# Weight sums of w_down made in place, products reordered, and seven products for two more tiles of gate and up

## The reference

```python
h = rms_norm(x, norm2[l])
x = x + (jax.nn.silu(h @ w_gate[l]) * (h @ w_up[l])) @ w_down[l]
return rms_norm(x, final_norm)
```

## Time and profile before

| | us |
|---|---|
| median of 3 runs | 660.89 |
| lowest, highest | 660.51, 661.07 |
| the profiled execution | 662.12 |
| its span, first to last instruction | 660.3 |
| TensorE busy | 646.7 (98% of the span) |
| VectorE busy | 451.1 (68%) |
| ScalarE busy | 348.5 (53%) |
| GpSimd busy | 265.0 (40%) |
| TensorE's granted clock, mean | 0.998 of full |

### The profile page before, as it was taken

One profiled execution on the slowest core, in us unless ns is written; L12 is line 12 of the kernel. 1 busy time (PEld: TensorE's weight loads), 2 busy tenths in 40 slices (PEclk: granted clock), 3 DMA queues, 4 the chain that ended last, 5 costly groups with the idle time before them and its releaser, 6 DMA issues.

```text
span 660.3 us, 11056 instructions
## 1 busy us (share of the span) xinstructions
PE 646.7 (98%) x3915; PEld 569.7 (86%) x3915; DVE 451.1 (68%) x929; ACT 348.5 (53%) x689; POOL 265.0 (40%) x158
## 2 busy tenths in 40 slices
PE   8999999999999999999999999999999999999996
PEld 7988988898899887888877888899999998888884
DVE  5435447555655687634489988469688797788894
ACT  7546446688665378715332362344444446655663
POOL 4766253674242440224466767344444320000222
PEclk9999999999999999999999999999999999999999
DMA  8989959469794993144699999887677858766553
GB/s 243 270 180 255 280 150 246 124 181 372 218 256 117 246 172 65 32 161 117 160 297 293 294 281 284 216 228 222 189 230 216 255 177 268 253 201 197 185 172 127
DMA packets 114774, 139.22 MB, mean 211 GB/s; under 512 B 5044, under 2 KB 74784, under 8 KB 114720
## 3 DMA queue, kind: packets, MB, share of 16 engines
q1 hardware_dynamic: 97880, 107.35, 51.9%
q0 software_dynamic: 14176, 26.64, 22.5%
q10 hardware_dynamic: 2664, 4.53, 2.0%
HBM read 132.19 MB, written 54.81 MB: 283 GB/s over the span
## 4 chain that ended last, share of the span: by engine, by line
PE 82%; issue 8%; POOL 6%; DVE 2%; ACT 1%; DMA 1%; POOLq 0%; SPq 0%; DVEq 0%; ACTq 0%
PE bank L776 8%; PE bank L778 8%; PE bank L777 8%; PE bank L795 7%; PE bank L797 7%; PE bank L796 7%; PE bank L1107 6%; PE bank L1105 6%; PE bank L1106 6%; PE bank L948 6%; POOL w_lo L728 4%; PE bank L924 3%; PE bank L908 2%; PE bank L909 2%; POOL down_sums L746 1%
## 5 line engine op out<-in xcount | busy, mean ns | idle before, releaser
L728 POOL TENSOR_TENSOR w_lo<-raw,w_hi 128x1024 fp32r<-128x1024 f32 (+1 forms) x76 | 191.6, 2525 | 259.4 <-ACT w_hi L1148 258.8
L1148 ACT CAST w_hi<-raw 128x1024 fp32r<-128x1024 f32 (+1 forms) x141 | 144.1, 1028 | 148.3 <-PE bank L1107 32.2
L795 PE MATMUL bank<-xT_hi,w_hi 128*128 128x512 f32 x272 | 109.0, 401 | 1.6 <-POOL w_lo L728 1.4
L797 PE MATMUL bank<-xT_hi,w_lo 128*128 128x512 f32 x272 | 107.0, 393 | 0.0
L796 PE MATMUL bank<-xT_lo,w_hi 128*128 128x512 f32 x272 | 106.7, 392 | 0.0
L1774 DVE TENSOR_TENSOR w_lo<-raw,w_hi 128x1024 fp32r<-128x1024 f32 x66 | 79.4, 1203 | 35.6 <-ACT w_hi L1148 35.2
L1617 DVE CUSTOM_DVE_ANT_0 bank<-bank,bias 128x128 f32<-128x128 f32 (+3 forms) x96 | 47.5, 497 | 75.0 <-PE bank L909 45.6
L795 PEld LDWEIGHTS bank<-xT_hi,w_hi 128*128 128x128 f32 x272 | 51.2, 188 | 12.8 <-POOL w_lo L728 1.7
L797 PEld LDWEIGHTS bank<-xT_hi,w_lo 128*128 128x128 f32 x272 | 51.1, 188 | 11.7
L1229 ACT ACTIVATE E<-bank,nmax 128x128 f32<-128x128 f32 (+3 forms) x80 | 42.4, 530 | 35.3 <-DVE nmax L1617 34.5
L796 PEld LDWEIGHTS bank<-xT_lo,w_hi 128*128 128x128 f32 x272 | 51.3, 188 | 9.7 <-issue 0.2
(11 more groups left out here) (280 smaller groups left out, 1607.8 us busy)
## 6 DMA issues: line engine op xcount, KB each, us to landing
raw<-mixed_sums SPq DMA_DIRECT2D x24, 512.0 KB, 5.0
raw<-in_w_gate_dram SPq DMA_DIRECT2D x22, 512.0 KB, 6.6
raw<-in_w_in_dram SPq DMA_DIRECT2D x20, 512.0 KB, 6.1
down_sums<-in_w_down_dram SPq DMA_DIRECT2D x20, 512.0 KB, 10.2
raw<-down_sums SPq DMA_DIRECT2D x20, 512.0 KB, 4.2
raw<-in_w_up_dram SPq DMA_DIRECT2D x16, 512.0 KB, 5.2
raw<-in_w_down_dram SPq DMA_DIRECT2D x15, 512.0 KB, 3.5
mixed_sums<-in_w_up_dram SPq DMA_DIRECT2D x12, 512.0 KB, 11.5
```

The lines of the kernel that those rows point to most:

```text
L728: nc.gpsimd.tensor_tensor(wv_lo(k)[:, 0:n], raw[:, k % RAW_SLOTS, 0:n], wv_hi(k)[:, 0:n].bitcast(F32), ALU.subtract).then_inc(s_split, 1)
L795: nc.tensor.matmul(bank[:, :], hi, xT_hi[:, kt, :], start=kt == 0, stop=False)
L797: return nc.tensor.matmul(bank[:, :], lo, xT_hi[:, kt, :], start=False, stop=kt == KT - 1)
L1148: nc.scalar.copy(wv_hi(k)[:, 0:n], raw[:, k % RAW_SLOTS, 0:n]).then_inc(s_whi, 1)
```

## The change

1. `F0` goes from 10 to 8. Tiles 8 and 9 leave the plain stage and become a seventh pair in the next. `RING`, the order of the PSUM banks in that stage, is turned so that its first banks are those which the plain tiles leave first.
2. The sums for gate and up cover 14 tiles instead of 12: 7 blocks for each T, 28 pieces in place of 24 (`BLOCKS`).
3. For w_down only T3 and T1 are copied and added as before (12 pieces). T2 is made in T3's place: once T3's chunk is loaded into `raw`, GpSimd adds w00 onto it. T4 is made in T2's place in the same way, by adding w10. These 12 adds have no copy; they stand in GpSimd's loop behind chunks (1, 3) to (2, 2) and (3, 3) to (5, 1) of w_down, but as GpSimd has nothing else to do there, each goes out when the chunk that it waits for has landed and the add four before it is done.
4. The products with w_down are reordered so that T3 comes at n = 1, T2 at n = 3 and T4 at n = 6. Only S2's result goes through `run`; VectorE makes 24 additions for products 0 to 5 in place of 22. `BACK` and `NORMED` follow the order.
5. Of the 40 copies, 24 lie ahead of the plain tiles, 12 with the 16 plain chunks (none at every fourth), and 4 in the seven-product stage.

```diff
-PRODUCTS = [(A11, ("w", 0, 0), 0), (S1, ("sum", T1), 1), (S2, ("sum", T2), 0), (A12, ("w", 1, 0), 2),
-            (S3, ("sum", T3), 0), (S4, ("w", 1, 1), 1), (A22, ("sum", T4), 0)]
+PRODUCTS = [(A11, ("w", 0, 0), 0), (S3, ("sum", T3), 1), (S1, ("sum", T1), 0), (S2, ("sum", T2), 2),
+            (A12, ("w", 1, 0), 0), (S4, ("w", 1, 1), 1), (A22, ("sum", T4), 0)]
-RUNNING = (2, 4)
+RUNNING = (3,)
-F0 = 10
+F0 = 8
+OF_DOWN = [(T3, (0, 1), ("w", 1, 1)), (T1, (0, 1), ("w", 0, 0)), (T2, T3, ("w", 0, 0)), (T4, T2, ("w", 1, 0))]
+PLACE = {T3: 0, T2: 0, T4: 0, T1: 1}
+BLOCKS = [(0, 4, 0, 2), (0, 4, 2, 2), (4, 4, 0, 2), (4, 4, 2, 2), (8, 4, 0, 2), (8, 4, 2, 2), (12, 2, 0, 4)]
-BACK = {(0, 5): (0, 0), (1, 1): (0, 1), (1, 3): (1, 1), (2, 1): (1, 0)}
+BACK = {(0, 5): (0, 0), (1, 1): (1, 1), (1, 3): (1, 0), (2, 1): (0, 1)}
...
-    copy_at += [n_fill + i for i in range(20)] + [n_fill + 2 * F0 + 4 + 10 * i for i in range(4)]
-    add_at = copy_at[0:16] + [31] * 8 + copy_at[24:]
+    copy_at += [n_fill + i for i in range(16) if i % 4 != 3] + [mixed0 + 4 + 10 * i for i in range(4)]
+    in_place = [down_from + GROUPS_M + 3 + i for i in range(6)] + [down_from + 3 * GROUPS_M + 3 + 2 * i for i in range(6)]
+    add_at = copy_at[0:16] + [31] * 8 + copy_at[24:] + in_place
...
-        RING = [ps[0], ps[6], ps[3], ps[4], ps[5], ps[2], ps[7], ps[1]]
+        RING = [ps[6], ps[3], ps[4], ps[5], ps[2], ps[0], ps[7], ps[1]]
...
-                kind, to, at_, _, add = todo[i]
-                pool.wait_ge(s_copied[i % 4], 16 * (i // 4 + 1))
+                kind, to, at_, begin, add = todo[i]
+                if i < len(copy_at):
+                    pool.wait_ge(s_copied[i % 4], 16 * (i // 4 + 1))
+                else:
+                    raw_landed(pool, index[("down", ([x_[1] for x_ in PRODUCTS].index(("sum", begin)), at_[0]))])
...
-            for k in range(down0):
+            for k in range(len(chunks)):
```

More of the change, by code:

```diff
@@ L115 @@
 T1, T3, T2, T4 = range(4)
-PRODUCTS = [(A11, ("w", 0, 0), 0), (S1, ("sum", T1), 1), (S2, ("sum", T2), 0), (A12, ("w", 1, 0), 2),
-            (S3, ("sum", T3), 0), (S4, ("w", 1, 1), 1), (A22, ("sum", T4), 0)]
+PRODUCTS = [(A11, ("w", 0, 0), 0), (S3, ("sum", T3), 1), (S1, ("sum", T1), 0), (S2, ("sum", T2), 2),
+            (A12, ("w", 1, 0), 0), (S4, ("w", 1, 1), 1), (A22, ("sum", T4), 0)]
 N_PROD = len(PRODUCTS)
-RUNNING = (2, 4)
-QUARTERS = [[(0, 0, 1)], [(1, 1, 1), (0, 1, 1)], [(0, 1, -1)], [(0, 0, 1)], [(1, 1, -1), (1, 0, 1)], [(0, 1, 1)], [(1, 0, 1)]]
+RUNNING = (3,)
+QUARTERS = [[(0, 0, 1)], [(1, 1, -1), (1, 0, 1)], [(1, 1, 1), (0, 1, 1)], [(0, 1, -1), (1, 1, -1), (1, 0, 1)], [(0, 0, 1)],
+            [(0, 1, 1)], [(1, 0, 1)]]
 GROUPS_M = 6
@@ L137 @@
 SUMS = [(T3, (0, 1), ("w", 1, 1)), (T1, (0, 1), ("w", 0, 0)), (T2, (0, 0), ("sum", T3)), (T4, (1, 0), ("sum", T2))]
-WIDE = 4
-BACK = {(0, 5): (0, 0), (1, 1): (0, 1), (1, 3): (1, 1), (2, 1): (1, 0)}
+OF_DOWN = [(T3, (0, 1), ("w", 1, 1)), (T1, (0, 1), ("w", 0, 0)), (T2, T3, ("w", 0, 0)), (T4, T2, ("w", 1, 0))]
+PLACE = {T3: 0, T2: 0, T4: 0, T1: 1}
+BLOCKS = [(0, 4, 0, 2), (0, 4, 2, 2), (4, 4, 0, 2), (4, 4, 2, 2), (8, 4, 0, 2), (8, 4, 2, 2), (12, 2, 0, 4)]
+BACK = {(0, 5): (0, 0), (1, 1): (1, 1), (1, 3): (1, 0), (2, 1): (0, 1)}
 X_FULL = {0: (0, 1, 2), 1: (3, 4, 5), 2: (6, 7)}
@@ L155, in plan_sums @@
     todo = []
-    for wides in ((0, 1), (2,)):
+    for blocks in ((0, 1, 2, 3), (4, 5, 6)):
         for to, begin, add in SUMS:
-            todo += [("mixed", to, (w_, kp), begin, add) for w_ in wides for kp in range(2)]
-    for to, begin, add in SUMS:
+            todo += [("mixed", to, (b,), begin, add) for b in blocks]
+    for to, begin, add in OF_DOWN:
         todo += [("down", to, (g,), begin, add) for g in range(GROUPS_M)]
@@ L219, in hymba_block @@
     todo = plan_sums()
+    mixed0, down_from = n_fill + 2 * F0, n_fill + 2 * F0 + N_UNIT * N_PAIR
     copy_at = [6 + i for i in range(10)] + [27 + i // 2 for i in range(14)]
-    copy_at += [n_fill + i for i in range(20)] + [n_fill + 2 * F0 + 4 + 10 * i for i in range(4)]
-    add_at = copy_at[0:16] + [31] * 8 + copy_at[24:]
+    copy_at += [n_fill + i for i in range(16) if i % 4 != 3] + [mixed0 + 4 + 10 * i for i in range(4)]
+    in_place = [down_from + GROUPS_M + 3 + i for i in range(6)] + [down_from + 3 * GROUPS_M + 3 + 2 * i for i in range(6)]
+    add_at = copy_at[0:16] + [31] * 8 + copy_at[24:] + in_place
+    assert len(add_at) == len(todo)
     by_dve = [c[0] == "down" or (c[0] == "mixed" and c[1][1] in BY_DVE) for c in chunks]
@@ L516, in hymba_block @@
         run = up_n
-        sums = nc.dram_tensor("down_sums", (len(SUMS), FP, P, 512), F32).ap()
+        sums = nc.dram_tensor("down_sums", (2, FP, P, 512), F32).ap()
         down0 = index[("down", (0, 0))]
-        NORMED = [(0, 0), (1, 0), (2, 1), (3, 1), (0, 1), (1, 1), (2, 0), (3, 0)]
+        NORMED = [(2, 1), (3, 1), (0, 0), (1, 0), (0, 1), (1, 1), (2, 0), (3, 0)]
         adds = [(n, rows_, dh, u) for n in range(N_PROD) for rows_, dh, _ in QUARTERS[n] for u in range(2)]
@@ L549, in part @@
             if what[0] == "sum":
-                return sums[what[1], m0:m1, :, :].rearrange("k p n -> p k n")
+                return sums[PLACE[what[1]], m0:m1, :, :].rearrange("k p n -> p k n")
             rows_, dh = what[1:]
@@ L568, in sum_part @@
                 return part(what, at_[0])
-            return mixed_part(what, F0 + WIDE * at_[0], WIDE, 2 * at_[1], 2)
+            f0, n, k0, n_k = BLOCKS[at_[0]]
+            return mixed_part(what, F0 + f0, n, k0, n_k)
         def sum_done(eng, kind, to, at_):
@@ L663, in _ @@
                     if UNITS[j][1][0] == "sum":
-                        for kp in range(2):
-                            sum_done(sp, "mixed", UNITS[j][1][1], (2 * p_ // WIDE, kp))
+                        for b, (f0, n, _, _) in enumerate(BLOCKS):
+                            if f0 <= 2 * p_ < f0 + n:
+                                sum_done(sp, "mixed", UNITS[j][1][1], (b,))
                     sp.dma_start(dst[:, 0:1024].rearrange("p (k n) -> p k n", k=4),
@@ L673, in _ @@
                     sp.dma_start(dst[:, 0:chunk_cols(k)].rearrange("p (k n) -> p k n", k=src.shape[1]), src).then_inc(signal, 16)
-                for i in [i for i in range(len(todo)) if copy_at[i] == k]:
+                for i in [i for i in range(len(copy_at)) if copy_at[i] == k]:
                     _, to, _, begin, _ = todo[i]
```

## The result

| | before | after |
|---|---|---|
| median (lowest to highest), same chip | 661.12 (660.51 to 661.86) | 676.26 (674.92 to 680.66) |
| ratio, 95% interval | | 1.023 (1.021 to 1.025) |
| the profiled execution | 662.12 | 675.4 |
| its span | 660.3 | 673.5 |
| first matmul of w_down | 547.23 | 544.06 |

15 us slower, against 3 forecast, and outside the range. The gain ahead of w_down is there; w_down loses 16.3 us, where part 5 took 6.0, with a range up to 9.1 and a further bound of 12.

A forecast was written before the change was run, and what follows sets the result against it. TensorE was taken to set the end, with DMA queues at their limit in the plain stage. Terms of -2.05 - 1.0 + 0 + 0 + 6.0 = +2.95 us on 660.9 gave 663.9 us, range 657.3 to 670.5.

The forecast's parts named there:

- part 5: w_down: the twelve adds in place delay loads and make TensorE wait 2.6 to 9.1 us, taken as 6.0.
- further bound of 12: w_down: if loads got only 86 GB/s beside adds, they fall behind by more than 10 us twice: 12 us.
- What bounds the kernel: TensorE, busy 98%, sets the end; DMA queues are full in the plain stage; VectorE is behind until x's forms are made.
- Parts 1 to 3: Before w_down: two tiles as a pair -2.05 us; fewer copies beside plain tiles -1.0 (0 to -1.4); earlier pair start 0.
- Rival C: First pair: VectorE is too late, costing 1 to 2.4 us at one place; chance 0.05.
- Part 4: w_down's reordered products: 24 VectorE additions for 22, up to eight in a row; cost 0, at most 1 us.
- The price of the DMAs: w_down: an add of 0.524 MB takes 2.55 us of the DMA engines, a load of the same size 1.50 us.
- The reserve: w_down's first burst: loads issued ahead of use have 4.4 to 7.4 us spare, set against 10 us too much DMA work.
- it wins back 1.8 per round, 3.6 in a product: w_down's product 2: three loads take 5.8 us against 7.6, so lead is regained before T4's adds, leaving waits of 0 to 3.5.
- rival B: w_down: loads are starved in both bursts of adds, +12 us, 669.9 us; chance 0.13.
- Rival A: w_down: adds are hidden in free DMA capacity and the loads' lead, 657.9 us; chance 0.24.
- rival D: w_down: waits come to 1 to 4 us and use up the gain, 660 us; chance 0.13.

The follow-up runs named there:

- The kernels with early copies: Changed kernel with T2 and T4 in places of their own, eight copies ahead of the plain tiles (behind chunk 36, then 37): 663.2 and 667.49 us.

## Why the prediction was wrong

*What bounds the kernel*: right for the changed kernel, whose whole loss came through late loads and, at one stop, VectorE. The kernels with early copies lost time in other ways too, GpSimd's own queue and a low granted clock.

*Parts 1 to 3*: right. The sum was -3.05 us up to w_down's start, measured 544.06 - 547.23 = -3.17. The plain stage ends at 403.79 (403.5 forecast), a pair is 20.03 us, both stops of the earlier trace rows are gone (the whole 1.4 us, where 1.0 was taken), and the first unit doesn't wait. Rival C falls.

*Part 4*: the cost of 0 holds when nothing else is late (no adds in place: 104.04 us). The "at most 1 us if low halves are late" was mis-sized: the condition came true and cost 2.9 us in the changed kernel, 3.1 with T4's adds alone. The additions and the low half behind them take 6.0 us (4.8 and 1.2) and a chunk 2.77, so once the lead of the low halves is used up the difference of 3.2 us can show, an estimate from these rows; I had set the additions against the whole product of 15.25 us instead.

*Part 5*: the chain of waits and the places right, the size wrong, 6.0 us (2.6 to 9.1) against 16.3, and with it the account of what makes a load late. Against the middles of the forecast the first burst cost 7.6 us for 4.1, the loads of the second 5.8 for 1.75, and the additions 2.9 for 0. Take the terms one by one.

- The price of the DMAs was nearly right. By the queues an add of 0.524 MB held the engines for 2.93 us (1.75 MB in 65.1% of 15 us). The 2.55 of the earlier trace rows is time by the clock at a share of 112.4%, so 2.87 in the same measure. A load held them for 1.46, against 1.53 by the earlier trace rows. For product 1 the queues give 27.0 us of engine time (16.1 + 8.0 + 2.9); at the full share of 1.09 the 15.25 us hold 16.6, so the excess stays at some 10 us, as forecast.
- The reserve was not. I subtracted 4.4 to 7.4 us from the first burst's excess. Lost were 7.6 us, 5.5 of them idle time (2.88, 1.71 and 0.89), so 2.4 to 4.5 were absorbed, depending on which of the two one sets against the excess: the lower end or less.
- The step that failed most is "it wins back 1.8 per round, 3.6 in a product", which gave the second burst a reserve of 3.6 to 7.4 us. Alone, T2's adds cost 7.3 us, and in the changed kernel 7.6 to the end of product 2: the waits run on into product 2 (stops at 586.38 and 591.71 us), which therefore wins nothing back. The second burst had an excess of 7.1 us by my own count. Alone it cost 5.2, of which the additions' stop is 3.1, so 2.1 for loads and 5.0 absorbed. Behind the first burst it cost 8.7, less 2.9 for the additions 5.8 for loads: 1.3 absorbed. One reserve was counted twice.
- The form of the sum fails too, work of the DMA engines above what they can do, less a reserve. With the adds paced it left 1 to 3 us of waits, and 13.3 us were lost with engines that were not full. A load beside an add lands late though the engines could do the work in the mean, and with three slots that alone holds back the next loads, once it takes more than the 6.0 us above. I had used the three slots for the round of three loads behind a burst (3.5 + 2.3), and not for the rounds during one. Why a load beside spaced adds takes 8.0 us isn't shown.
- Not counted at all: what follows a stop. After the 2.88 us at 572.02 the matmuls start 0.43 us apart instead of 0.23:

```profile
572.02 0.80 PE L789 MATMUL bank<-w_hi,high 128*128 128x512 f32 x1 [2.88 <-DVE w_lo L1787]
572.61 0.63 PE L790 MATMUL bank<-w_lo,high 128*128 128x512 f32 x1
573.04 0.63 PE L791 MATMUL bank<-w_hi,form_lo_b 128*128 128x512 f32 x1
573.47 0.63 PE L789 MATMUL bank<-w_hi,high 128*128 128x512 f32 x1
```

This cost some 1.3 us there, and each of the eight stops takes some 0.27 us beyond its idle time, as the matmuls beside it are drawn out. Idle time is 12.8 of the 16.3 us, this the other 3.5. In the first burst the 5.5 us of idle time lie inside the 2.6 to 5.6 that the sum had for its waits, and 2.1 us came on top.

The terms as measured: 7.6 in the first burst, 5.8 for loads and 2.9 for the additions in the second, 16.3. The last two are what the 8.7 was divided into, so this is an account of the loss and not a test of it.

*The bounds.* The upper end of 12 us came from the earlier trace rows, 86 GB/s for loads beside several adds. Measured were 121 GB/s of weights, a milder starvation, and still more loss, since I let the adds last 19 us a burst and be over. They go out as chunks land, so the slower the loads, the longer the adds are there: the first burst's went out from 551 to 574 us, the second's from 592 to 612. In rival B I had held this against it ("later loads make later adds"), as a brake on the loss; it only spread it. Rival A asked for loads that keep 189 GB/s beside adds and falls with the 121; rival D asked for waits of 1 to 4 us and falls with the 16.3. The Trainium skill (DMA: Bandwidth & Descriptors, section Queues, rings and completion order) lets the queues of an engine take turns by packet, and what it calls a packet is typically a group of 9 to 17 descriptors. No run shows whether the profile's packets, of 1.9 KB here, are the same thing. The rows of after show something near to equal turns: 913 adding packets and 1229 others of the same size. But equal turns are equal bytes, not equal time, and an adding packet holds the engine twice as long (65.1% for 913, 43.5% for 1229). I had read the rule as an add's own length laid once on each load; it is laid on every load that runs while adds are out.

*The chances.* 0.60 on slower was the right side. The range ended at B's centre, and nothing in it stood for two bursts that share one reserve.

## What to carry over

A lead of buffered chunks is a stock, not a rate: write down where it is spent, and give a second burst only what the time between them can win back. Before adding up the engines' work, ask how long a load may take: slots times the time of a chunk, less the time to empty a slot (here 8.3 - 2.3 = 6.0 us), and look up how late loads land beside such a DMA. Then ask for each stage that uses a chunk in under 3 us how many background DMAs it bears: beside the pairs a copy and an add in every sixth chunk were free and in every third cost 11.5 us; in w_down twelve adds cost 16.3 us at one a chunk, and 13.3 at one in two or three. Work that was free beside early operands (a run of additions) has a price as soon as these are late, and it is the longest step without a new operand that sets it.

## What the runs showed of the hardware

- An accumulating DMA from HBM to HBM holds the DMA engines about twice as long per byte as a plain one: 179 against 403 GB/s of engine time, at the same place and size. The plain copies on SyncE's queue, with 1.5 KB to a packet, went at 376. In w_down the twelve adds cost 16.3 us where plain DMAs of the same bytes cost 1.9 to 2.9.
- The loads beside them landed after 9.5 us (median) with adds, 8.0 with the adds paced, 6.0 and 5.4 with plain DMAs and 4.0 with neither, all issued from 555 to 575 us.
- TensorE's clock fell after some of its stops. From 570 to 575 us of the changed kernel the granted clock was 0.66, and matmuls came at 0.43 us, the pace of the lower level (1.2 GHz), for six matmuls after 2.88 us of idle time; after 3.37 us at 572.23 (T2's adds alone) for some nine. After 2.14 us at 656.30 (adds paced) there were some eight, with a granted clock of 0.66 from 656 to 661. After 2.93 us at 630.89 and 3.09 us at 619.13 (T4's adds alone) there was no such stretch, so the length of the stop doesn't settle it alone.
- With the DMA engines full in the attention stage TensorE stood 1.81 us with no releaser that the profile shows ("issue"), seen in one execution. What held it wasn't tried.
